# Turning the weights of two key tiles together, in every second slot of the stick-breaking stage

## The chip, the cores and the metric

The kernel runs on one core of a Trainium2 chip. The metric is the device time of one execution in microseconds (us). Five engines work side by side, each through its own list of instructions in order, and they wait for one another with semaphores: TensorE (PE in the profile, its weight loads PEld), VectorE (DVE), ScalarE (ACT), GpSimd (POOL) and SyncE (SP), which here issues the DMA transfers.

## The reference, cut to what matters

One layer of a streaming encoder for 2048 prompt frames and 32 sample frames. The part that the change touches is the stick-breaking attention of the prompt: 8 heads of 64, no softmax.

```python
def stick_breaking(q, k, v, q_pos, k_pos):
    z = jnp.einsum('bqhd,bkhd->bhqk', q, k).astype(jnp.float32) * (HEAD_DIM ** -0.5)
    mask = k_pos[None, :] < q_pos[:, None]
    log_keep = jnp.where(mask, jax.nn.log_sigmoid(-z), 0.0)
    after = lax.cumsum(log_keep, axis=3, reverse=True) - log_keep
    w = jnp.where(mask, jnp.exp(jax.nn.log_sigmoid(z) + after), 0.0)
    return jnp.einsum('bhqk,bkhd->bqhd', w.astype(v.dtype), v)
```

The weight of a key is sigmoid(z) times the product of sigmoid(-z) over all keys after it. Around it stand an input projection, a sliding-window attention, gates, and `x + mixed @ w_out`.

## The kernel before, in words

The program first norms and projects (norm, window and pair stages), then does the sample frames, and from 712 us on runs the stick-breaking stage, which the change edits. It takes the prompt in four blocks of 512 queries. For each block and head it goes back over the key blocks from the diagonal one (`u.diagonal`) to the first (`u.last`). One head with one query block and one key block is a *unit*: 80 in all, of four *tiles* each, so 320 tiles, numbered c. A diagonal unit has narrower tiles.

A tile goes through six steps on four engines:

1. `front` (PE): two products give scores in `c_score`, L1527 and L1528; a diagonal unit adds a mask, L1530.
2. `sigmoids` (ACT): *keep*, L1381, and *take*, L1384.
3. `scan` (DVE): the running product from the last key to the first, L1462.
4. `weigh` (POOL): take times the scanned product, into `c_weight`, L1356.
5. `turn` (PE): transposes of 128x128, L1539. Steps 1 to 4 are by 128 queries, and a turn is by 128 keys, so it reads all four query tiles of its unit. ACT copies the turned tile rounded into `c_w_hi` (`back_hi`, L1392), and DVE puts the rest into `c_w_lo` (`back_lo`, L1470).
6. `mix` (PE): the weights' two parts times the values, summed over a head in `c_o`, L1552 and L1553. At a head's end ACT and DVE take the sum out (`finish`, L1397 and L1475), and the first `mix` of the next head waits for that (`o_ready`).

The order on each engine is written out by hand, by a loop over *slots*. In slot c TensorE does `turn(c)`, `front(c + 8)`, one to five *flow* pieces, and `mix(c - 3)`. The flow is other matrix work woven in: the gates' projection and the output projection (L1572 to L1574, a step of three products with 512 or 272 columns), and transposes of its results (L1587). ACT does in slot c `back_hi(c)` and `sigmoids(c + 8)`, then the flow's copies and, every four to eight slots, the rounding of new flow weights (L1130). DVE does `scan(c + 7)`, `back_lo(c)`, then the flow's sums; POOL does `weigh(c + 5)`, the gating product (L1363) and the rest of the flow weights (L1134).

The turned tiles alternate between two PSUM banks, `turn_ps[c % 2]`, and so do the scores. The waits that matter here:

- `turn(c)` waits for `back_lo(c - 2)` (which frees its bank), and with the first tile of a unit for all four `weigh` of the unit.
- `front(c)` waits for `scan(c - 2)`.
- `back_hi(c)` waits for `turn(c)` and for `mix(c - 4)`.
- The first `weigh` of unit u waits until the last tile of unit u - 2 is turned; take of tile c waits for `weigh(c - 4)`.

Of the kernel before, what the change touches and what calls it, by code (L numbers as in the profile page):

```python
# [254 lines left out]
def after(eng, signal, count):  # L255

    if count > 0:
        eng.wait_ge(signal, count)
# [727 lines left out]
SB_SLOTS = PHASE_START[NSB]  # L986
# [165 lines left out]
def stick_breaking_stage(nc, s, flow):  # L1152
# [13 lines left out]
    with ExitStack() as ctx:  # L1166
# [349 lines left out]
        def _(pe):  # L1516
            def front(c):
                u, j = UNITS[c // QB], c % QB
                after(pe, take_ready, c - 1)
                after(pe, scanned, c - 1)  # L1520
                if j == 0:
                    if u.diagonal:
                        pe.wait_ge(flow.q_in[u.e], 32 * (u.head // 2 + 1))
                    pe.wait_ge(flow.k_in[u.number % 3], 16 * (u.number // 3 + 1))
                n = u.width(j)
                out, keys = score[c % 2][:, 0:n], flow.k[u.number % 3][:, 0:n]
                pe.matmul(out, flow.q[u.e][:, 0, P * j:P * j + P], keys, start=True, stop=False)  # L1527
                last = pe.matmul(out, flow.q[u.e][:, 1, P * j:P * j + P], keys, start=False, stop=not u.diagonal)  # L1528
                if u.diagonal:
                    last = pe.matmul(score[c % 2][:, n - P:n], s.ident_r[:], s.causal_r[:], start=False, stop=True)  # L1530
                last.then_inc(scored, 1)

            def turn(c):
                u, n = UNITS[c // QB], c % QB
                if n == 0:
                    pe.wait_ge(weighted, 4 * u.number + 4)
                after(pe, lo_ready, c - 1)
                for j in range(n if u.diagonal else 0, QB):
                    last = pe.transpose(turn_ps[c % 2][:, j * P:(j + 1) * P],  # L1539
                                        weight[:, u.number % 2, j, n * P:(n + 1) * P], s.ident[:])  # L1540
                last.then_inc(turned, 1)

            def mix(c):
                u, n = UNITS[c // QB], c % QB
                pe.wait_ge(lo_ready, c + 1)
                if n == 0:
                    if u.diagonal:
                        after(pe, o_ready, u.head)
                    pe.wait_ge(flow.v_in[u.number % 3], 16 * (u.number // 3 + 1))
                cols = slice(P * n if u.diagonal else 0, SB)  # L1550
                v = flow.v[u.number % 3][:, n, :]
                pe.matmul(o_ps[:, cols], v, w_hi[n][:, cols], start=(u.diagonal and n == 0), stop=False)  # L1552
                pe.matmul(o_ps[:, cols], v, w_lo[n][:, cols], start=False, stop=(u.last and n == QB - 1)).then_inc(mixed, 1)  # L1553

            def flow_atom(p, nth):

                dt = MIX_ORDER[nth]
                j = p.chunk
                cols = slice(p.first, p.first + p.cols)
                if p.kind == GATE:  # L1560
                    xh, xl = (a[min(p.b, 1)][:, dt, cols] for a in (flow.hi, flow.lo))
                else:
                    xh, xl = (a[mix_home(p.b)][:, dt, cols] for a in (flow.hi, flow.lo))
                if nth == 0:
                    after(pe, flow_free[p.bank], p.turn)
                    pe.wait_ge(flow.w_lo_ready, j + 1)
                    if p.kind == GATE and p.m == 0 and p.b:
                        pe.wait_ge(flow.x_in[p.b], 16 * 2 * DT)
                if p.kind == OUT and p.m == 0:
                    pe.wait_ge(m_lo_ready, DT * p.b + nth + 1)  # L1570
                out = flow_ps[p.bank][:, 0:p.cols]
                pe.matmul(out, flow.w_hi[j % 3][:, dt, :], xh, start=(nth == 0), stop=False)  # L1572
                pe.matmul(out, flow.w_hi[j % 3][:, dt, :], xl, start=False, stop=False)  # L1573
                last = pe.matmul(out, flow.w_lo[j % 3][:, dt, :], xh, start=False, stop=(nth == DT - 1))  # L1574
                if nth == DT - 1:
                    last.then_inc(flow_ready, 1)

            def flow_rows(p):

                after(pe, flow_free[p.bank], p.turn)  # L1580
                sources = [outs[p.b, p.m, f] for f in ((0, 272) if p.b == 0 else (0,))] if p.kind == ROWS else \
                          [outs[p.b, DT - 1, 272]]
                for src in sources:
                    pe.wait_ge(flow_free[src.bank], src.turn + 1)
                for j in range(QB):
                    if p.kind == ROWS:
                        last = pe.transpose(flow_ps[p.bank][:, j * P:(j + 1) * P], part[p.m % 2][:, j * P:(j + 1) * P],  # L1587
                                            s.ident[:])
                    else:
                        last = pe.transpose(flow_ps[p.bank][0:NS, j * P:(j + 1) * P], ys[:, QB * p.m + j, :], s.ident[:])  # L1590
                last.then_inc(flow_ready, 1)

            for c in range(SLOT_0, SLOTS_ALL):
                if 0 <= c < SB_SLOTS:
                    turn(c)
                if c + 8 < SB_SLOTS:
                    front(c + 8)
                for p in pieces:
                    for nth, slot in enumerate(p.slots):
                        if slot == c:  # L1600
                            if p.kind in (GATE, OUT):
                                flow_atom(p, nth)
                            else:
                                flow_rows(p)
                if 0 <= c - 3 < SB_SLOTS:
                    mix(c - 3)
# [347 lines left out]
```

## Time and profile before

| | |
|---|---|
| median of 3 runs | 1534.36 us (1531.79 to 1536.13) |
| profiled execution | 1534.72 us, span in the trace 1532.9 us |
| PE busy over the span | 1392.3 us (91%) |
| DVE, ACT, POOL busy | 1031.1 us (67%), 896.0 us (58%), 580.6 us (38%) |
| granted TensorE clock, mean | 0.96 |

Busy is the time in which an engine has an instruction running. The matmuls of PE overlap, so two that start 0.23 us apart are each shown as 0.39 us long. The times in the rows below are from the start of the span.

### The profile page before, as it was taken

How to read it: one execution, taken by the hardware profiler on the slowest of the kernel's cores; microseconds unless marked ns; L12 is line 12 of the kernel's file. 1: busy time of each engine (PE TensorE's matmuls, PEld its weight loads, DVE VectorE, ACT ScalarE, POOL GpSimd, SP SyncE). 2: the span in 40 equal slices, each digit the busy share in tenths (PEclk: the TensorE clock that was granted, in tenths of full speed). 3: DMA queues.
4: the chain of work that ended last, by engine and by line, in shares of the span. 5: the costliest groups of instructions: out<-in, count | busy, mean ns of one | idle time of the engine just before them, and what ended most of it. 6: DMA issues, size and time to landing. Idle time of an engine off the chain costs nothing.

```text
span 1532.9 us, 23564 instructions
## 1 busy us (share of the span) xinstructions
PE 1392.3 (91%) x7794; PEld 1182.7 (77%) x7794; DVE 1031.1 (67%) x1467; ACT 896.0 (58%) x1927; POOL 580.6 (38%) x481
## 2 busy tenths in 40 slices
PE   3699986998999999868999999899999999999988
PEld 2588875887877887748987899687888777777767
DVE  5467752767567666544777766688887898888931
ACT  7433332555545555325776676577777787777831
POOL 1010111110110101024467645566565666655742
PEclk9699997999999999968999999999999999999999
DMA  5045544554545555364978677655675655445533
GB/s 223 28 180 222 194 139 143 165 155 139 160 131 157 156 150 140 122 171 125 270 239 250 181 217 198 179 175 165 191 213 153 191 173 144 128 124 149 170 119 110
DMA packets 267487, 254.37 MB, mean 166 GB/s; under 512 B 22401, under 2 KB 198137, under 8 KB 266601
## 3 DMA queue, kind: packets, MB, share of 16 engines
q1 hardware_dynamic: 267368, 252.88, 55.5%
q8 instruction: 64, 1.05, 0.3%
q14 instruction: 55, 0.44, 0.1%
HBM read 165.84 MB, written 87.16 MB: 165 GB/s over the span
## 4 chain that ended last, share of the span: by engine, by line
PE 38%; issue 7%; POOL 5%; ACT 2%; DVE 1%; DMA 1%; POOLq 0%; SPq 0%; DVEq 0%; ACTq 0%
PE c_flow L1572 6%; PE c_flow L1574 6%; PE c_flow L1573 6%; PE c_turn L1539 6%; POOL c_weight L1356 3%; PE c_score L1527 3%; PE c_o L1552 3%; PE c_score L1528 3%; PE c_o L1553 3%; POOL f_w_lo L1134 1%; ACT cache_k_rows L1384 1%; PE c_flow L1587 1%; DVE f_kept L1462 1%; POOL c_o_in L1363 1%; ACT f_keep L1381 1%
## 5 line engine op out<-in xcount | busy, mean ns | idle before, releaser
L1356 POOL TENSOR_TENSOR c_weight<-cache_k_rows,f_kept 128x512 f32<-128x512 f32 (+2 forms) x320 | 306.6, 985 | 91.6 <-PE c_turn L1539 82.1
L1462 DVE TENSOR_TENSOR_SCAN f_kept<-f_keep,f_kept,c_score 128x513 f32<-128x513 f32 x192 | 245.1, 1276 | 45.4 <-ACT cache_k_rows L1384 39.0
L1470 DVE TENSOR_TENSOR c_w_lo<-c_turn,c_w_hi 128x512 fp32r<-128x512 f32 (+1 forms) x320 | 191.8, 599 | 80.6 <-ACT c_w_hi L1392 77.8
L1392 ACT ACTIVATE c_w_hi<-c_turn 128x512 fp32r<-128x512 f32 (+1 forms) x320 | 171.4, 536 | 127.3 <-PE c_turn L1539 123.9
L1134 POOL TENSOR_TENSOR f_w_lo<-f_w_raw,f_w_hi 128x1024 fp32r<-128x1024 f32 x64 | 153.5, 2400 | 211.2 <-ACT f_w_hi L1130 211.2
L248 POOL TENSOR_TENSOR w_w_lo<-w_w_raw,w_w_hi 128x1024 fp32r<-128x1024 f32 x18 | 44.0, 2444 | 392.5 <-ACT w_w_hi L243 392.3
L1384 ACT ACTIVATE cache_k_rows<-c_score 128x512 f32<-128x512 f32 (+2 forms) x320 | 173.1, 541 | 33.2 <-POOL c_weight L1356 33.0
L276 PE MATMUL b_ps<-XH,w_w_hi 128*128 128x512 f32 (+1 forms) x480 | 178.3, 371 | 11.4 <-PEq L290 11.4
L1539 PE MATMUL c_turn<-ident,c_weight 128*128 128x128 f32 x1088 | 173.5, 275 | 5.9 <-POOL c_weight L1356 3.0
L1381 ACT ACTIVATE f_keep<-c_score 128x512 f32<-128x512 f32 (+2 forms) x320 | 171.0, 534 | 10.5 <-PE c_score L1530 5.2
L278 PE MATMUL b_ps<-XH,w_w_lo 128*128 128x512 f32 (+1 forms) x480 | 170.3, 355 | 0.0
L277 PE MATMUL b_ps<-XL,w_w_hi 128*128 128x512 f32 (+1 forms) x480 | 170.1, 354 | 0.0
L1539 PEld LDWEIGHTS c_turn<-ident,c_weight 128*128 128x128 f32 x1088 | 134.6, 141 | 38.4 <-POOL c_weight L1356 6.4
L1527 PE MATMUL c_score<-f_k,f_q 128*128 128x512 f32 (+2 forms) x320 | 142.9, 447 | 13.8 <-DVE f_kept L1462 8.2
L1552 PE MATMUL c_o<-c_w_hi,f_v 128*128 128x512 f32 (+1 forms) x320 | 118.5, 370 | 16.0 <-issue 15.5
L1572 PE MATMUL c_flow<-XH,f_w_hi 128*128 128x272 f32 (+1 forms) x384 | 130.1, 339 | 0.0
L1462 DVE TENSOR_TENSOR_SCAN f_kept<-f_keep,c_score 128x128 f32<-128x128 f32 (+3 forms) x128 | 104.4, 816 | 36.9 <-ACT cache_k_rows L1384 32.1
L1574 PE MATMUL c_flow<-XH,f_w_lo 128*128 128x272 f32 (+1 forms) x384 | 125.3, 326 | 0.0
L1573 PE MATMUL c_flow<-XL,f_w_hi 128*128 128x272 f32 (+1 forms) x384 | 125.1, 326 | 0.0
L1528 PE MATMUL c_score<-f_k,f_q 128*128 128x512 f32 (+2 forms) x320 | 117.9, 368 | 0.0
L1553 PE MATMUL c_o<-c_w_lo,f_v 128*128 128x512 f32 (+1 forms) x320 | 117.6, 367 | 0.0
L1572 PE MATMUL c_flow<-f_hi,f_w_hi 128*128 128x512 f32 x256 | 104.9, 410 | 7.8 <-DVE f_lo L1496 6.3
(227 smaller groups left out, 3152.0 us busy)
## 6 DMA issues: line engine op xcount, KB each, us to landing
f_k<-k_parts SPq DMA_DIRECT2D x80, 256.0 KB, 4.1
f_v<-v_parts SPq DMA_DIRECT2D x80, 256.0 KB, 2.7
f_q<-q_parts SPq DMA_DIRECT2D x64, 256.0 KB, 5.3
f_w_raw<-in_w_in SPq DMA_DIRECT2D x32, 512.0 KB, 4.2
f_w_raw<-in_w_out SPq DMA_DIRECT2D x32, 512.0 KB, 4.1
w_w_raw<-in_w_in SPq DMA_DIRECT2D x18, 512.0 KB, 4.7
x_rows<-in_x_prompt SPq DMA_DIRECT2D x4, 2048.0 KB, 10.1
k_parts<-b_part SPq DMA_DIRECT2D x16, 512.0 KB, 2.8
```

Source lines behind the costliest of these rows:

```text
L276: pe.matmul(out, w.hi[n][:, dt, :], xh, start=(dt == 0), stop=False)
L1356: pool.tensor_tensor(weight[:, u.number % 2, j, 0:n], take[:, j, 0:n], kept[:, j, 1:n + 1], ALU.mult).then_inc(weighted, 1)
L1381: act.activation(keep[:, c % 2, 0:n], score[c % 2][:, 0:n], ACT.Sigmoid, scale=-SCALE)\
L1384: act.activation(take[:, j, 0:n], score[c % 2][:, 0:n], ACT.Sigmoid, scale=SCALE)\
L1392: act.activation(w_hi[n][:, cols], turn_ps[c % 2][:, cols], ACT.Copy).then_inc(hi_ready, 1)
L1462: dve.tensor_tensor_scan(kept[:, j, down], keep[:, c % 2, down], score[c % 2][:, 0:1].to_broadcast([P, n]), above, ALU.mult, ALU.bypass).t ...
L1470: dve.tensor_tensor(w_lo[n][:, cols], turn_ps[c % 2][:, cols], f32(w_hi[n][:, cols]), ALU.subtract).then_inc(lo_ready, 1)
L1527: pe.matmul(out, flow.q[u.e][:, 0, P * j:P * j + P], keys, start=True, stop=False)
L1539: last = pe.transpose(turn_ps[c % 2][:, j * P:(j + 1) * P], weight[:, u.number % 2, j, n * P:(n + 1) * P], s.ident[:])
L1572: pe.matmul(out, flow.w_hi[j % 3][:, dt, :], xh, start=(nth == 0), stop=False)
L1573: pe.matmul(out, flow.w_hi[j % 3][:, dt, :], xl, start=False, stop=False)
L1574: last = pe.matmul(out, flow.w_lo[j % 3][:, dt, :], xh, start=False, stop=(nth == DT - 1))
```

## The change

In even slots TensorE turns tile c and then tile c + 1; in odd slots it turns none. Everything else in TensorE's list, and all of the other engines' lists, stays as it is, and no wait is added to or taken from an instruction. `turn(c + 1)` is the same list of transposes with the same waits, but it stands ahead of `front(c + 8)`, of the flow work of slot c, of `mix(c - 3)` and of whatever slot c has else, all of which stood ahead of it before.

```diff
@@ -1591,8 +1591,9 @@
             for c in range(SLOT_0, SLOTS_ALL):
-                if 0 <= c < SB_SLOTS:
+                if 0 <= c < SB_SLOTS and c % 2 == 0:
                     turn(c)
+                    turn(c + 1)
                 if c + 8 < SB_SLOTS:
                     front(c + 8)
                 for p in pieces:
```

The first place is slots 236 and 237 on TensorE, full-width tiles of the last query block, before the change. `c_turn0` and `c_turn1` are the two banks of turned tiles, `c_score0` and `c_score1` those of the scores, and the semaphore `c_lo_ready` counts `back_lo`, `c_scanned` counts `scan`.

```order
5920 L1539 MATMUL c_turn0<-ident,c_weight 128x128 [waits c_lo_ready,c_weighted]
5921 L1539 MATMUL c_turn0<-ident,c_weight 128x128 x3
5922 L1527 MATMUL c_score0<-f_k1,f_q1 128x512 [waits f_k_in1,c_scanned,c_take_ready]
5923 L1528 MATMUL c_score0<-f_k1,f_q1 128x512
5924 L1572 MATMUL c_flow1<-f_hi,f_w_hi0 128x512
5925 L1573 MATMUL c_flow1<-f_lo,f_w_hi0 128x512
5926 L1574 MATMUL c_flow1<-f_hi,f_w_lo0 128x512
5927 L1552 MATMUL c_o<-c_w_hi1,f_v1 128x512 [waits c_lo_ready]
5928 L1553 MATMUL c_o<-c_w_lo1,f_v1 128x512
5929 L1539 MATMUL c_turn1<-ident,c_weight 128x128 [waits c_lo_ready]
5930 L1539 MATMUL c_turn1<-ident,c_weight 128x128 x3
5931 L1527 MATMUL c_score1<-f_k1,f_q1 128x512 [waits c_scanned,c_take_ready]
```

The same place on TensorE in the changed kernel:

```order
5920 L1539 MATMUL c_turn0<-ident,c_weight 128x128 [waits c_lo_ready,c_weighted]
5921 L1539 MATMUL c_turn0<-ident,c_weight 128x128 x3
5922 L1539 MATMUL c_turn1<-ident,c_weight 128x128 [waits c_lo_ready]
5923 L1539 MATMUL c_turn1<-ident,c_weight 128x128 x3
5924 L1527 MATMUL c_score0<-f_k1,f_q1 128x512 [waits f_k_in1,c_scanned,c_take_ready]
5925 L1528 MATMUL c_score0<-f_k1,f_q1 128x512
5926 L1572 MATMUL c_flow1<-f_hi,f_w_hi0 128x512
5927 L1573 MATMUL c_flow1<-f_lo,f_w_hi0 128x512
5928 L1574 MATMUL c_flow1<-f_hi,f_w_lo0 128x512
5929 L1552 MATMUL c_o<-c_w_hi1,f_v1 128x512 [waits c_lo_ready]
5930 L1553 MATMUL c_o<-c_w_lo1,f_v1 128x512
5931 L1527 MATMUL c_score1<-f_k1,f_q1 128x512 [waits c_scanned,c_take_ready]
```

The four transposes of `turn(237)`, with their wait for `back_lo(235)`, have moved from behind `mix(233)` to ahead of `front(244)`; the score products, the flow step and the mix of slot 236 now come after it, and slot 237 begins with its score products.

The second place is the end of a head on TensorE, slots 110 and 111 before the change: 4660 and 4661 are the last mix of a head, 4671 the first of the next, which waits for `c_o_ready`.

```order
4660 L1552 MATMUL c_o<-c_w_hi3,f_v2 128x512 [waits c_lo_ready]
4661 L1553 MATMUL c_o<-c_w_lo3,f_v2 128x512
4662 L1539 MATMUL c_turn1<-ident,c_weight 128x128 [waits c_lo_ready]
4663 L1527 MATMUL c_score1<-f_k2,f_q1 128x512 [waits c_scanned,c_take_ready]
4664 L1528 MATMUL c_score1<-f_k2,f_q1 128x512
4665 L1572 MATMUL c_flow1<-f_hi,f_w_hi2 128x512
4666 L1573 MATMUL c_flow1<-f_lo,f_w_hi2 128x512
4667 L1574 MATMUL c_flow1<-f_hi,f_w_lo2 128x512
4668 L1572 MATMUL c_flow1<-f_hi,f_w_hi2 128x512
4669 L1573 MATMUL c_flow1<-f_lo,f_w_hi2 128x512
4670 L1574 MATMUL c_flow1<-f_hi,f_w_lo2 128x512
4671 L1552 MATMUL c_o<-c_w_hi0,f_v0 128x512 [waits f_v_in0,c_o_ready,c_lo_ready]
```

In the changed kernel TensorE's list from `turn(110)` on reads:

```order
4653 L1539 MATMUL c_turn0<-ident,c_weight 128x128 [waits c_lo_ready]
4654 L1539 MATMUL c_turn0<-ident,c_weight 128x128
4655 L1539 MATMUL c_turn1<-ident,c_weight 128x128 [waits c_lo_ready]
4656 L1527 MATMUL c_score0<-f_k2,f_q1 128x512 [waits c_scanned,c_take_ready]
4657 L1528 MATMUL c_score0<-f_k2,f_q1 128x512
4658 L1572 MATMUL c_flow1<-f_hi,f_w_hi2 128x512
4659 L1573 MATMUL c_flow1<-f_lo,f_w_hi2 128x512
4660 L1574 MATMUL c_flow1<-f_hi,f_w_lo2 128x512
4661 L1552 MATMUL c_o<-c_w_hi3,f_v2 128x512 [waits c_lo_ready]
4662 L1553 MATMUL c_o<-c_w_lo3,f_v2 128x512
4663 L1527 MATMUL c_score1<-f_k2,f_q1 128x512 [waits c_scanned,c_take_ready]
4664 L1528 MATMUL c_score1<-f_k2,f_q1 128x512
```

The single transpose that stood between the last mix of the old head and the first of the new one now stands ahead of both.

## Rows read from the trace of the kernel before

**Rows 1.** Windows: length; busy of PE, PEld, DVE, ACT, POOL; clock; DMA

```profile
963.00:1194.00 231.00, 218.64 (x1167) 180.20 (x1165) 180.87 (x225) 169.88 (x336) 140.02 (x120) 0.98 0.61 179
1194.00:1472.00 278.00, 260.75 (x1408) 212.12 (x1407) 240.98 (x290) 215.22 (x424) 181.95 (x154) 1.00 0.52 152
...
990.00:995.00 5.00, 2.42 (x7) 1.80 (x8) 3.66 (x4) 2.70 (x6) 3.60 (x5) 0.50 0.65 210
```

**Rows 2.** Waits, 712 to 1533 us: who for whom, us in total, times, longest

```profile
ACT c_w_hi L1392 <- PE c_turn L1539: 123.9, 175, 2.9
POOL c_weight L1356 <- PE c_turn L1539: 82.1, 35, 6.2
DVE c_w_lo L1470 <- ACT c_w_hi L1392: 77.8, 113, 5.0
...
ACT cache_k_rows L1384 <- POOL c_weight L1356: 33.0, 38, 2.0
...
PE c_o L1552 <- issue: 15.5, 17, 2.0
...
PE c_score L1527 <- DVE f_kept L1462: 8.2, 11, 2.6
...
PE c_turn L1539 <- POOL c_weight L1356: 3.0, 6, 0.9
```

**Rows 3.** Timeline of PE around `turn(111)`, a single transpose

```profile
1007.36 0.27 PE L1539 MATMUL c_turn<-ident,c_weight 128*128 128x128 f32 x1
...
1007.38 0.48 PE L1527 MATMUL c_score<-f_k,f_q 128*128 128x512 f32 x1
...
1007.70 0.40 PE L1528 MATMUL c_score<-f_k,f_q 128*128 128x512 f32 x1
```

**Rows 4.** Timeline, slots 236 to 238: PE, ACT and DVE

```profile
1293.48 0.60 PE L1539 MATMUL c_turn<-ident,c_weight 128*128 128x128 f32 x4
...
1294.15 0.39 PE L1528 MATMUL c_score<-f_k,f_q 128*128 128x512 f32 x1
...
1297.61 0.60 PE L1539 MATMUL c_turn<-ident,c_weight 128*128 128x128 f32 x4
...
1294.60 0.59 ACT L1381 ACTIVATE f_keep<-c_score 128x512 f32<-128x512 f32 x1
1295.08 0.61 ACT L1384 ACTIVATE cache_k_rows<-c_score 128x512 f32<-128x512 f32 x1
...
1295.78 1.28 DVE L1462 TENSOR_TENSOR_SCAN f_kept<-f_keep,f_kept,c_score 128x513 f32<-128x513 f32 x1 [0.34 <-ACT cache_k_rows L1384]
1296.98 0.66 DVE L1470 TENSOR_TENSOR c_w_lo<-c_turn,c_w_hi 128x512 fp32r<-128x512 f32 x1
```

**Rows 5.** Timeline, slots 46 and 318: PE, and the back_lo needed

```profile
822.80 0.60 PE L1539 MATMUL c_turn<-ident,c_weight 128*128 128x128 f32 x4
...
827.81 0.47 PE L1527 MATMUL c_score<-f_k,f_q 128*128 128x512 f32 x1 [1.92 <-DVE f_kept L1462]
...
823.93 0.69 DVE L1470 TENSOR_TENSOR c_w_lo<-c_turn,c_w_hi 128x512 fp32r<-128x512 f32 x1 [3.19 <-ACT c_w_hi L1392]
...
1469.39 0.66 PE L1539 MATMUL c_turn<-ident,c_weight 128*128 128x128 f32 x4
...
1469.85 0.68 DVE L1470 TENSOR_TENSOR c_w_lo<-c_turn,c_w_hi 128x512 fp32r<-128x512 f32 x1
```

**Rows 6.** Timeline at the head's end in slot 111: DVE, then PE

```profile
1009.53 0.68 DVE L1475 TENSOR_TENSOR c_o_sum<-c_o,c_o_sum 64x512 f32<-64x512 f32 x1
...
1010.32 0.47 PE L1552 MATMUL c_o<-c_w_hi,f_v 128*128 128x512 f32 x1 [0.84 <-issue]
```

**Rows 7.** Timeline of POOL, one unit and a half of the last block

```profile
1350.28 2.41 POOL L1134 TENSOR_TENSOR f_w_lo<-f_w_raw,f_w_hi 128x1024 fp32r<-128x1024 f32 x1 [4.39 <-ACT f_w_hi L1130]
1352.64 5.30 POOL L1356 TENSOR_TENSOR c_weight<-cache_k_rows,f_kept 128x512 f32<-128x512 f32 x5
1360.56 1.85 POOL L1356 TENSOR_TENSOR c_weight<-cache_k_rows,f_kept 128x128 f32<-128x128 f32 x3 [2.61 <-PE c_turn L1539]
```

## The prediction

> **What bounds the kernel now.** I read the windows first. In the last query block of the stick-breaking stage (1194 to 1472 us, 128 slots) PE is busy 260.75 of 278 us, DVE 240.98 and ACT 215.22; in the block before it the shares are 95%, 78% and 74% [rows 1]. So TensorE sets the pace, and in the last block DVE is close behind: there is little room for PE and DVE to get out of step. Then the waits. PE waits little in the stage: 15.5 us at the ends of heads (shown as "issue"; the wait is for the head's sum, below), 8.2 us for a scan, 3.0 us for POOL before a turn. The large waits are on engines that are ahead: POOL for a turn 82.1 us, ACT for a turn 123.9 us of the same kind (of which nothing here depends), DVE for ACT's rounded half 77.8 us [rows 2]. Last I read the timeline slot by slot, for what a turned tile waits for and how long before the turn that was ready.
>
> **The transposes themselves: nothing.** Grouping could pay if each switch between transposes and products cost something. At turn(111), one transpose, the second score product starts 0.34 us after it; at turn(236), four transposes, 0.67 us after the first [rows 3, 4]. Three more transposes cost 0.33 us, 0.11 each, and 0.34 - 0.11 = 0.23 is what one 512-column product takes to the start of the next. The line goes through zero: no fixed cost per group, so 160 fewer groups save 0. A turn of four is 0.45 us, and it is done once, before and after.
>
> **The wait that moves.** turn(c + 1) needs back_lo(c - 1). That used to be asked at the start of slot c + 1, a slot of some 2.1 us later; now it is asked right behind turn(c). On DVE back_lo(c - 1) comes directly after scan(c + 6), so TensorE must now wait in slot c until DVE has done that scan and one subtraction more, where before only front(c + 8) asked for the scan alone. Queued behind the wait are front(c + 8), the flow step and mix(c - 3), and for the scores ACT, DVE and POOL wait in turn.
>
> I went through all 159 even slots from c = 2 and compared the end of back_lo(c - 1) with the end of turn(c) (start plus 0.11 per transpose). It is late in 25: 1 in the second query block, 4 in the third, 20 in the last, 1.38 + 5.37 + 8.86 = 15.6 us in all. The first is slot 46: turn at 822.80, ended 823.24, subtraction ended 824.62, 1.38 late. The last is slot 318: 1469.39 + 0.44 against 1470.53, 0.70 late [rows 5]. In 31 more it is ready by less than 0.45 us.
>
> Term 1, the 25 late places. They don't all cost. In six of them front(c + 8) already waits in the same slot for the scan just ahead of that subtraction, 4.65 us, and at slots 46 (1.38) and 232 (0.45) a longer wait follows in the next slot and shrinks by as much: 1.92 us at 827.81 [rows 5]. That leaves 15.6 - 4.65 - 1.83 = 9.1. Where several follow within a few slots it is one lag of DVE seen again, and TensorE pays for its largest once: 2.5 less. **+6.6 us**; bounds 0 (all trades against later waits) and 15.6.
>
> Term 2, the shift. In even slots front(c + 8) now starts 0.45 us later, behind the second turn, and the subtraction that the next pair needs hangs on it. Slots 236 to 238 show the loop: scores end 1294.15 + 0.39 = 1294.54, take ends 1295.69, the scan starts 1295.78, the subtraction ends 1297.64, 3.10 us after the scores; turn(238) starts 1297.61 [rows 4]. With the scores 0.45 us later the subtraction ends 1298.09, and turn(239) could go at 1297.61 + 0.45 = 1298.06. With 0.06 us for the semaphore (as from the scores' end to ACT at 1294.60) TensorE stalls 0.1 us, in the plainest pair of full slots (4.13 us a pair), and more wherever DVE has an extra sum or a take is late. For the 31 places with little room, 0.51 less the room of each sums to 7.6 us, and where ACT or DVE was behind anyway the later scores are hidden: I take half, 3.8. The late places get the shift too, at most 25 x 0.5 = 12.7; most of them are late because DVE or ACT is behind, so I take 1.7. **+5.5 us**; bounds 0 and 20.3. In odd slots front moves not at all: what its slot loses at the head the slot before gained.
>
> Term 3, the ends of heads. The last mix of a head is in an even slot and the first of the next in the odd one behind it. ACT copies, DVE adds until 1010.21, PE starts at 1010.32 after 0.84 idle [rows 6]. The one transpose between the two mixes now stands ahead of both, so it no longer covers 0.11 us of this. 17 such waits [rows 2]: **+1.9 us**; bounds 0 and 2.
>
> Term 4, what comes back. ACT may round an odd tile at once when its slot begins, some 0.45 us earlier than now, so DVE gets odd tiles earlier where it waits for ACT: a part of the 77.8 us [rows 2]. POOL's first weigh of a unit is released a slot earlier. Little of this reaches PE, since take and scan of odd tiles hang on scores that don't move. **-3 us**, an estimate; bounds 0 and -12 (the faster rival).
>
> The DMAs, ACT's, DVE's and POOL's lists are untouched. Sum: 6.6 + 5.5 + 1.9 - 3 = +11 us, on the profiled execution 1534.72 + 11 = 1545.7. That execution is 0.36 us above the median, so **1545.4 us** against 1534.36.
>
> **Rivals.** *The waits only trade* (0.23). DVE's list is the same and PE waited for its scans anyway; a stall lets DVE, ACT and POOL catch up, and the next stall shrinks. For it: slot 46, and the other seven places above. Against it: PE waits only 8.2 us for scans in all [rows 2], less than the 15.6 us that comes, so at least the rest is new. Terms 1 and 2 at a quarter, 3.0, plus 1.9, less the 3: about +2, 1536 us.
>
> *Faster: POOL released early* (0.10). The 82.1 us in which POOL waits for the last turn of a unit [rows 2] end a slot sooner. If that made weights and so takes earlier, it would eat ACT's 33.0 us of waits for POOL, then PE's 3.0 for POOL and 8.2 for scans [rows 2], together 11.2; less term 3, and with terms 1 and 2 traded away, -9: 1525 us. Against it: in the last block POOL is late just after it took the flow weights at 1350.28, held 4.39 us by ACT and not by a turn, then runs five weighs on end; where it waits for a turn, 2.61 us before 1360.56, it is ahead [rows 7]. It decides if more than about a third of ACT's 38 waits come from POOL runs that a turn released; I found none in the last block.
>
> *Slower by the clock* (0.04). The granted clock is 1.00 over the whole last block, with a turn's 0.45 us in each slot; it was seen at 0.50 (1.2 GHz) around 990 to 995 us, where PE was busy 2.42 of 5 us [rows 1]. If pairs of turns with a stall behind turn(c) let it fall once more for two stretches of ten microseconds, that is 10 us on top: 1556 us. The Trainium skill, "TensorE: Matmul & The Clock Gate", in its part on PE-mode transpose, says that transposes don't count as busy as matmuls do, which would speak against eight in a row. The window of the last block, a fifth of it transposes at full clock, doesn't bear that out, and the share stays the same.
>
> My forecast, a new wait of TensorE for DVE, has the rest, 0.63.
>
> **How the numbers follow.** Within 0.3% of the old median (4.6 us, about what a measurement tells from no change) is 1529.8 to 1539.0. The forecast's own range is 1537 (term 2 nearly nothing) to 1557 (term 1 at 9, term 2 at twice, nothing back); a tenth of it falls under 1539. Slower: 0.57 + 0.04 and 0.05 of the trading rival, 0.66. Same: 0.06 + 0.16 + 0.02 of the faster rival, 0.24. Faster: 0.08 + 0.02 of trading, 0.10. The range takes in the trading rival and stops short of the faster one: 1532 to 1557.
>
> **What the changed profile would show.** Right: in PE's waits a large group c_turn <- DVE c_w_lo, 10 us or more, nearly all after 963 us and in even slots, while c_score <- DVE shrinks to a few us; the wait "issue" before c_o 1 to 2 us larger; POOL's wait for a turn well under 82 us with no gain on PE; the last block some 8 us longer than now, the first two no longer. The transposes still 0.11 us apart. Wrong: c_turn <- DVE stays under 5 us, or it comes and as much goes elsewhere; or the waits of POOL and ACT fall and PE's with them; or the clock falls in the last block.

## The result

The changed kernel takes **1545.31 us** (median of 4 runs, 1544.43 to 1547.6) against 1533.97 us before (4 runs on the same chip, 1531.79 to 1536.13): ratio 1.0076, 95% interval 1.0058 to 1.0094. It is slower by some 11 us; the forecast was 1545.4. The profiled execution took 1545.52 us, with a span of 1543.7 us.

Busy time over the span, from the page of the changed kernel, hardly moved against the table of before. TensorE does the same work over a longer time:

```profile
PE 1395.5 (90%) x7794; PEld 1187.0 (77%) x7794; DVE 1030.5 (67%) x1467; ACT 902.6 (58%) x1927; POOL 581.3 (38%) x481
```

The waits of the changed kernel, 712 to 1545 us (who for whom, us in total, times, longest), which answer to [rows 2]:

```profile
ACT c_w_hi L1392 <- PE c_turn L1539: 55.2, 88, 2.0
POOL c_weight L1356 <- PE c_turn L1539: 31.0, 18, 3.9
DVE c_w_lo L1470 <- ACT c_w_hi L1392: 67.3, 96, 3.9
...
ACT cache_k_rows L1384 <- POOL c_weight L1356: 30.2, 37, 2.1
ACT f_keep L1381 <- PE c_score L1528: 28.3, 72, 2.4
...
PE c_o L1552 <- issue: 17.9, 19, 2.3
...
PE c_turn L1539 <- DVE c_w_lo L1470: 15.9, 20, 3.5
...
PE c_turn L1539 <- POOL c_weight L1356: 2.3, 5, 0.8
...
PE c_score L1527 <- DVE f_kept L1462: 1.3, 4, 0.4
```

In the trace of before, the same wait of TensorE for DVE's subtraction was:

```profile
PE c_turn L1539 <- DVE c_w_lo L1470: 2.7, 2, 2.6
```

Three things are to be seen. TensorE has a new wait, a turn that waits for DVE's subtraction: 15.9 us in 20 places, against 2.7 us in 2. Its wait for a scan fell from 8.2 to 1.3 us, so about 6.9 us of the new wait were there already under another name. And POOL's wait for a turn fell from 82.1 to 31.0 us, ACT's for a turn from 123.9 to 55.2, while ACT's wait for POOL only went from 33.0 to 30.2: those engines get turned tiles earlier and it brings TensorE nothing.

Where the time went is told by marks, each the start of an instruction: the first scores of the stage (at 696.2 us in the trace of before, so the stage starts somewhat earlier than the 712 us given at its description), `turn(192)`, which opens the last query block, and the last `mix`. "Last block" is from `turn(192)` to the last `mix`. "To the end" runs on to the end of the span, some 60 us later.

| us | first scores to turn(192) | last block | first scores to the end |
|---|---|---|---|
| before | 498.0 | 278.8 | 836.7 |
| changed | 497.9 | 288.3 | 846.6 |

The two rows that bound the last block, in the trace of before and in that of the changed kernel:

```profile
1194.18 0.60 PE L1539 MATMUL c_turn<-ident,c_weight 128*128 128x128 f32 x4
...
1472.97 0.50 PE L1552 MATMUL c_o<-c_w_hi,f_v 128*128 128x512 f32 x1 [0.36 <-DVE c_w_lo L1470]
```

```profile
1195.01 0.93 PE L1539 MATMUL c_turn<-ident,c_weight 128*128 128x128 f32 x7
...
1483.32 0.50 PE L1552 MATMUL c_o<-c_w_hi,f_v 128*128 128x512 f32 x1
```

The last block is 9.5 us longer. The stretch before it is as long as it was, but that hides a loss of about 2 us, as the traces taken again will show. Tile by tile, the mix of a tile comes 0.3 us earlier than before at tile 96, then 0.9 us later at tile 192, 4.9 at 224, 7.7 at 256, 8.6 at 288 and 10.4 at 319: a loss spread over the whole block. The granted clock has a small part in it. The windows that answer to [rows 1] show 0.99 in both blocks, where before had 0.98 and 1.00:

```profile
963.00:1194.00 231.00, 217.29 (x1161) 180.21 (x1159) 179.59 (x224) 170.06 (x334) 139.58 (x119) 0.99 0.60 178
1195.00:1483.00 288.00, 266.30 (x1409) 215.40 (x1407) 242.24 (x291) 218.36 (x424) 181.79 (x153) 0.99 0.49 148
```

One place shows the mechanism at its plainest. The timeline of the changed kernel from slot 260 on, where turns 260 and 261 stand together:

```profile
1352.79 1.03 PE L1539 MATMUL c_turn<-ident,c_weight 128*128 128x128 f32 x8
...
1353.58 0.48 PE L1527 MATMUL c_score<-f_k,f_q 128*128 128x512 f32 x1
...
1353.90 0.40 PE L1528 MATMUL c_score<-f_k,f_q 128*128 128x512 f32 x1
...
1354.34 0.60 ACT L1381 ACTIVATE f_keep<-c_score 128x512 f32<-128x512 f32 x1 [0.31 <-PE c_score L1528]
1354.83 0.59 ACT L1384 ACTIVATE cache_k_rows<-c_score 128x512 f32<-128x512 f32 x1
1355.51 1.28 DVE L1462 TENSOR_TENSOR_SCAN f_kept<-f_keep,f_kept,c_score 128x513 f32<-128x513 f32 x1 [0.77 <-ACT cache_k_rows L1384]
1356.71 0.67 DVE L1470 TENSOR_TENSOR c_w_lo<-c_turn,c_w_hi 128x512 fp32r<-128x512 f32 x1
...
1356.58 0.60 PE L1539 MATMUL c_turn<-ident,c_weight 128*128 128x128 f32 x4
...
1357.43 0.66 PE L1539 MATMUL c_turn<-ident,c_weight 128*128 128x128 f32 x4 [0.25 <-DVE c_w_lo L1470]
```

Eight transposes, then the scores; ACT waits 0.31 us for them and DVE 0.77 us for ACT; the subtraction behind that scan ends at 1357.38, and the second turn of the next pair starts at 1357.43, 0.85 us after the first, where four transposes take 0.44. Before the change that subtraction had ended 0.07 us before the first turn did. Measured like this, from start to start and less 0.109 us per transpose, TensorE loses 20.7 us between the two turns of a pair in the whole stage, in 49 places: 2.1 in the second query block, 5.2 in the third and 13.5 in the last. That is more than the wait rows show, since the modelled ends of matmuls hide the start of each gap.

### The profile page after: what moved, and what is told of

Same layout as the page of the kernel before. It is cut to its first block, busy times and chain, and to the rows that moved or that the text cites. A ratio compares the mean times of both kernels' runs of the same rounds, so it can differ in the third digit from the quotient of the medians.

```text
span 1543.7 us, 23564 instructions
## 1 busy us (share of the span) xinstructions
PE 1395.5 (90%) x7794; PEld 1187.0 (77%) x7794; DVE 1030.5 (67%) x1467; ACT 902.6 (58%) x1927; POOL 581.3 (38%) x481
## 4 chain that ended last, share of the span: by engine, by line
PE 38%; issue 6%; POOL 4%; ACT 4%; DVE 2%; DMA 1%; SPq 0%; DVEq 0%; ACTq 0%; POOLq 0%
PE c_flow L1572 6%; PE c_turn L1539 6%; PE c_flow L1573 6%; PE c_flow L1574 6%; PE c_score L1527 3%; PE c_score L1528 3%; PE c_o L1552 3%; PE c_o L1553 3%; POOL c_weight L1356 2%; ACT cache_k_rows L1384 1%; ACT f_keep L1381 1%; POOL c_o_in L1363 1%; PE c_flow L1587 1%; ACT c_w_hi L1392 1%; POOL f_w_lo L1134 1%
## 5 line engine op out<-in xcount | busy, mean ns | idle before, releaser
L1392 ACT ACTIVATE c_w_hi<-c_turn 128x512 fp32r<-128x512 f32 (+1 forms) x320 | 171.5, 536 | 101.6 <-PE c_turn L1539 55.2
L1384 ACT ACTIVATE cache_k_rows<-c_score 128x512 f32<-128x512 f32 (+2 forms) x320 | 172.1, 538 | 30.4 <-POOL c_weight L1356 30.2
L1539 PE MATMUL c_turn<-ident,c_weight 128*128 128x128 f32 x1088 | 153.9, 276 | 18.6 <-DVE c_w_lo L1470 15.9
L1539 PEld LDWEIGHTS c_turn<-ident,c_weight 128*128 128x128 f32 x1088 | 126.7, 141 | 46.6 <-DVE c_w_lo L1470 24.2
L1527 PE MATMUL c_score<-f_k,f_q 128*128 128x512 f32 (+2 forms) x320 | 131.7, 412 | 6.1 <-PEq L1616 3.9
L1552 PE MATMUL c_o<-c_w_hi,f_v 128*128 128x512 f32 (+1 forms) x320 | 118.3, 370 | 18.1 <-issue 17.9
L1528 PE MATMUL c_score<-f_k,f_q 128*128 128x512 f32 (+2 forms) x320 | 117.9, 369 | 0.0
## 6 DMA issues: line engine op xcount, KB each, us to landing
x_rows<-in_x_prompt SPq DMA_DIRECT2D x4, 2048.0 KB, 10.3
```

Of the source, the lines that this page charges most:

```text
L1384: act.activation(take[:, j, 0:n], score[c % 2][:, 0:n], ACT.Sigmoid, scale=SCALE)\
L1392: act.activation(w_hi[n][:, cols], turn_ps[c % 2][:, cols], ACT.Copy).then_inc(hi_ready, 1)
L1539: last = pe.transpose(turn_ps[c % 2][:, j * P:(j + 1) * P], weight[:, u.number % 2, j, n * P:(n + 1) * P], s.ident[:])
```

## The experiments

The expectations name three theories. W: the time goes where TensorE waits for DVE's subtraction behind an early turn, and late scores feed back into that wait. S: the late scores alone starve ACT and DVE. T: transposes in a group, or the clock, cost TensorE itself. In the tables "last block" and "to the end" are the two stretches above. Since one trace each is compared, I first give what two runs of the same kernel differ by.

**Both kernels again.** No edit.

> The kernel before once more with a profile, to see how far two traces of one kernel differ: first score to the end of the span 836.7 us in the first, last query block 278.8. I expect within 1.5 and 0.7 us of these.

> The changed kernel once more with a profile, for the same reason: 846.6 us and 288.3 us in the first, within 1.5 and 0.7 us of these.

| | first to turn(192) | last block | to the end | lost in the last block |
|---|---|---|---|---|
| before, again | 495.7 | 280.2 | 836.1 | 29.2 |
| changed, again | 497.5 | 289.0 | 846.4 | 38.1 |

"Lost" is the last block less what its matmuls take at their plain spacing from start to start, about 251 us in every kernel; the first traces gave 27.7 and 37.5. The stretch to the end repeats within 0.6 us, the last block within 1.4 (more than I had expected), and the first three blocks only within 2.3. The single times, 1532.85 and 1540.46 us, differ from the medians by more: the first scores start anywhere from 689 to 701 us, behind stages that no edit touches. Means of the two are used for "to the end" below: 836.4 and 846.5.

Much of this scatter goes with the granted clock. In the last block, the second trace of before has a stretch of 3.4 us at a granted 0.50 (1.2 of 2.4 GHz), which the first lacks. Its row, in the order of [rows 1]:

```profile
1237.00:1240.00 3.00, 3.00 (x11) 2.51 (x11) 3.00 (x4) 1.48 (x3) 2.28 (x2) 0.50 0.70 197
```

It comes just after TensorE stood idle for 2.02 us at a head's end. The first trace of before has the same wait, 2.04 us at the same place, and its clock stays at 1.00. So such a stretch comes and goes between runs of one kernel, and a trace is best compared with one that spent as long at 0.50 in the same blocks:

| order of turns | first to turn(192), us of it at 0.50 | last block, us of it at 0.50 |
|---|---|---|
| old: before | 498.0, 20.0 | 278.8, 0 |
| old: before, again | 495.7, 12.9 | 280.2, 3.4 |
| old in the first three blocks, pairs in the last (below) | 495.2, 10.1 | 289.4, 3.4 |
| pairs in the first three blocks, old in the last (below) | 498.0, 10.1 | 278.2, 0 |
| pairs: changed | 497.9, 10.1 | 288.3, 3.4 |
| pairs: changed, again | 497.5, 10.1 | 289.0, 3.4 |

Like with like, the pairs cost 8.1 to 8.8 us in the last block (against 280.2) and some 2 us in the first three (497.5 to 498.0 against 495.2, and 496.4 in the kernel with the third bank and the old order, which also has 10.1 us). Traces with the same order and the same time at 0.50 differ by 1.2 us or less. The differences of the last block in brackets below are against the trace of before with the same time at 0.50 there.

The timed runs show it too. Of 34 timed runs of the kernel before on one chip, the 15 with a mean clock up to 0.960 took 1537.9 us on average and the 12 with 0.965 or more 1529.6. A straight line through time and mean clock, the same for an edited kernel and for before, gives each edit's difference "at equal clock". It is an estimate from the timed runs of both kernels, uncertain by about 1.3 us to either side for kernels with 10 runs or more and by up to 2 for those with six.

**The second turn behind the scores.** Turns stay paired in even slots, but `front(c + 8)` stands between them. The edit is shown against the kernel before.

```diff
-                if 0 <= c < SB_SLOTS:
+                if 0 <= c < SB_SLOTS and c % 2 == 0:
                     turn(c)
                 if c + 8 < SB_SLOTS:
                     front(c + 8)
+                if 0 <= c < SB_SLOTS and c % 2 == 0:
+                    turn(c + 1)
```

> In even slots TensorE turns tile c, then does the scores of tile c + 8, then turns tile c + 1; the rest is as in the change. The scores of even slots are no longer late, and the early turn asks for its subtraction 0.46 us later than in the change. Theory W (the time goes where TensorE, behind the early turn, waits for DVE's subtraction of tile c - 1, with the late scores feeding back into that wait): most of it comes back, a few places over half a us late stay, 1535 to 1539 us. Theory S (the late scores of even slots alone starve ACT and DVE, the subtraction wait only shows it): all comes back, 1533 to 1535. Theory T (transposes grouped two and two, or the clock, cost TensorE itself): 1534. If the time stays at 1543 or more, what counts is only that the odd turn stands in the even slot, and W's feedback is wrong.

Ratio 1.0005 (0.9982 to 1.0027), at equal clock -0.5 us; last block 278.5 (-0.3), to the end 835.4. Its waits on TensorE:

```profile
PE c_score L1527 <- DVE f_kept L1462: 7.8, 10, 3.0
...
PE c_turn L1539 <- DVE c_w_lo L1470: 4.3, 5, 2.6
```

The early second turn costs nothing once the scores go ahead of it. POOL's wait for a turn is 30.8 us here too, and no gain is to be seen from that relief either. This removes two causes: the second turn's place a slot earlier, and the flow and mix that now stand behind it. What costs is its place ahead of the scores. Eight transposes in a row are not tested here, since the scores part them; their spacing and the kernel with wait and late scores, below, speak to that.

**The wait alone.** The old order; in even slots TensorE asks behind `turn(c)` for what `turn(c + 1)` would ask.

```diff
                     turn(c)
+                    if c % 2 == 0 and c:
+                        pe.wait_ge(lo_ready, c)
```

> The order of before, with one more wait: in even slots the scores of tile c + 8 also wait until DVE has done the subtraction of tile c - 1. Nothing is moved, so the scores are late only where they wait. Theory W: the late places cost without the feedback of 0.45 us, 4 to 7 us, 1538 to 1541. Theory S: nothing or up to 2 us, 1534 to 1536. Theory T: nothing, 1534.

Ratio 1.0046 (1.0026 to 1.0067), at equal clock +5.8 us, in theory W's range; last block 282.9 (+2.7), to the end 842.1 (+5.7). The scores now wait for the subtraction:

```profile
PE c_score L1527 <- DVE c_w_lo L1470: 8.7, 9, 3.5
...
PE c_score L1527 <- DVE f_kept L1462: 1.9, 5, 0.6
```

The wait costs without any transpose moved, and takes over most of the 8.2 us for scans.

**The scores late alone.** The old order of turns; in even slots, except at the ends of heads, `mix(c - 3)` (0.46 us) goes ahead of `front(c + 8)`. This shifts the scores by what the second turn does, and adds no wait.

```diff
+            def early(c):
+                return c % 2 == 0 and not ((c - 3) % QB == QB - 1 and UNITS[(c - 3) // QB].last)
 ...
+                if 0 <= c - 3 < SB_SLOTS and early(c):
+                    mix(c - 3)
                 if c + 8 < SB_SLOTS:
                     front(c + 8)
 ...
-                if 0 <= c - 3 < SB_SLOTS:
+                if 0 <= c - 3 < SB_SLOTS and not early(c):
                     mix(c - 3)
```

> The order of before, turns where they stood, but in even slots (those at a head's end left out) mix(c - 3) is done before the scores of tile c + 8 instead of at the slot's end, so that these scores start 0.46 us late, as in the change, with no early turn and no new wait. In the trace the last query block (mix of tile 191 to mix of tile 319) took 272.7 us before and 281.9 with the change. Theory W (the late scores cost only because the early turn's subtraction hangs on them): 272 to 275 us there, the whole 1533 to 1537 us. Theory S (the late scores alone starve ACT and DVE): 277 to 282 us there, the whole 1540 us or more.

Ratio 1.005 (1.0026 to 1.0073), at equal clock +3.9 us; last block 281.3 (+1.1), to the end 842.5 (+6.1). By the expectation's own mark, from the mix of tile 191 to that of tile 319, the last block takes 275.2 us, at the edge of what theory W said; the whole time is what theory S said, so neither held. Late scores cost something by themselves, and more of it in the first three blocks (500.3 us, with 20.1 at 0.50, against 498.0 with 20.0), which I can't lay on one wait. The mix itself moved too, so this isn't a pure shift of the scores.

**Wait and late scores together**, the two edits above in one kernel, turns unmoved.

> No turn is moved. In even slots (at the ends of heads without the second part) the wait of e4_wait_only for the subtraction of tile c - 1 is put in, and mix(c - 3) stands between it and the scores of tile c + 8, as in e10_scores_late. Alone, the wait cost 4.1 us in the last query block and the late scores 2.5; the change cost 9.5. Theory W (the two feed each other: the subtraction hangs on scores that are late by its own wait): 8 to 11 us there, as in the change, though all transposes stand where they stood. If the two merely add: 6 to 7. If 5 or less, something else of the pair (the transposes themselves) makes up the difference.

Ratio 1.008 (1.0055 to 1.0105), at equal clock +10.8 us; last block 286.6 (+7.8), to the end 846.8 (+10.4). The loss of the changed kernel is there, within the noise, without a single transpose moved. The wait now shows at the mix, which is first behind it:

```profile
PE c_o L1552 <- issue: 17.1, 17, 2.5
PE c_o L1552 <- DVE c_w_lo L1470: 12.1, 15, 3.5
```

By the expectation's numbers, 7.8 us lies between adding (6 to 7) and feeding each other (8 to 11). Like with like it speaks for feeding: this trace has nothing at 0.50 in the last block and the other two have 3.4 us, and 2.7 + 1.1 = 3.8 us apart stand against 7.8 together, where equal traces differed by at most 1.2. Over the whole nothing of the kind is to be seen: 5.8 + 3.9 = 9.7 us apart against 10.8, at equal clock. That each feeds the other is likely for the last block, then, but it rests on one trace of each kernel.

**By blocks.** The pairs only in the last query block (`c >= PHASE_START[3]`), and only before it.

```diff
+                if 0 <= c < SB_SLOTS and (c < PHASE_START[3] or c % 2 == 0):
                     turn(c)
+                    if c >= PHASE_START[3]:
+                        turn(c + 1)
```

> Turns in pairs only from slot 192 on, the last query block. Theory W: nearly the whole loss is here, where DVE has little room (20 of the 25 late places): the last block takes 280 to 283 us, the whole is 8 to 10 us over the kernel before. A theory in which each pair costs the same wherever it stands (T, or a cost of the switch of banks) gives 64 of 160 pairs, 4 to 5 us.

> Turns in pairs only before slot 192, the first three query blocks, 96 of 160 pairs. Theory W: 0 to 2 us over the kernel before, and the last block 272 to 274 us. A theory in which each pair costs the same gives 6 to 7 us.

| | ratio | at equal clock | last block | to the end | `c_turn` for `back_lo` |
|---|---|---|---|---|---|
| last block only | 1.0065 (1.0033 to 1.0097) | +9.0 us | 289.4 (+9.2) | 843.8 | 10.3 us |
| first three only | 1.0033 (1.0009 to 1.0058) | +2.8 us | 278.2 (-0.6) | 836.4 | 7.1 us |

The expectations count the last block from mix to mix, as above (272.7 us before, 281.9 changed); so counted it takes 283.2 and 272.1 us here, as theory W said to within 0.2. Most of the loss is in the last block, and pairs don't cost the same wherever they stand. The first three blocks cost little, though they have 7.1 us of the new wait: the wait for a scan fell from 8.2 to 3.5 us there. That the stretch to the end is no longer than before, 836.4 us, goes with the clock: at equal time at 0.50 these blocks take some 2 us more (the table above), and the timed runs at equal clock say 2.8. The ratio's 0.3% is less firm than it looks, since the medians are 1534.89 and 1534.29.

**A third bank for turned tiles.** With three banks `turn(c + 1)` asks for `back_lo(c - 2)`, a slot less late. The third is taken from the flow in the last block alone; a control has the same banks and the old order. Two lines of the edit:

```diff
+        turn_bank = lambda c: turn_ps[c % 2] if c < LAST else (turn_ps + [flow_ps[2]])[c % 3]
 ...
-                after(pe, lo_ready, c - 1)
+                after(pe, lo_ready, c - 2 if c >= LAST + 3 else c - 1)
```

> The change, and in the last query block (slots 192 to 319) the turned tiles rotate through three PSUM banks, the third taken from the flow, which there has two instead of three. So in that block turn(c + 1) asks for the subtraction of tile c - 2, not c - 1; the scores of even slots stay 0.45 us late. To be read against e6_banks_plain. Theory W: the difference to e6 is 1 to 4 us (the loss of the first blocks, 1 to 2, and the heads' ends, 1). Theory S and theory T: it stays about 11 us.

> The order of before with the same three banks for turned tiles and two for the flow in the last block: the control of e5. The flow may wait for ACT's copies where its bank comes back sooner, the turns wait less: 1533 to 1542 us. All theories say the same of it; what counts is e5 less this.

| | time, us (before 1536.32) | last block | lost there |
|---|---|---|---|
| pairs, third bank | 1543.46, 1.0059 (1.0037 to 1.0082) | 284.6 | 33.8 |
| old order, third bank | 1539.62, 1.0035 (1.0014 to 1.0056) | 280.8 | 30.0 |

```profile
PE c_turn L1549 <- DVE c_w_lo L1478: 6.8, 4, 3.6
...
PE c_score L1535 <- DVE f_kept L1470: 5.1, 12, 0.7
```

Neither trace has time at 0.50 in the last block. Pairing costs that block 3.8 us over its control instead of 8.1 to 8.8, and all of the 6.8 us of the wait for the subtraction lie before it: in the last block, where the changed kernel has 8.1 us of that wait, there is none. Taking the early wait away takes more than half of the loss there away. What is left, 3.8, is more than late scores alone cost there (+1.1); I have no trace that tells the rest. Over the whole the difference is less clear: 3.8 us by the medians, as theory W said, but 5.9 at equal clock and 8.3 to the end in the two traces (845.1 and 836.8), since the first three blocks are paired in one and not in the other.

**The ends of heads.** In the slot of a head's last mix, that mix goes ahead of `front`: `early(c)` is now true at the ends of heads and nowhere else.

```diff
+            def early(c):
+                return (c - 3) % QB == QB - 1 and UNITS[(c - 3) // QB].last
```

> The order of before, but the last mix of each head stands ahead of the scores of its slot instead of at the slot's end, so that the head's sum is out before the next head's first mix asks for it. By term 3 read the other way (what stands between the last mix and the next head's first covers the wait), the 15.5 us of waits before c_o should fall to under 3, and 5 to 14 us come off: 1520 to 1529 us, unless waits for scans take their place (the scores of these slots start 0.2 to 0.4 us late), in which case 1532 to 1536.

Ratio 1.003 (1.0008 to 1.0053), at equal clock +3.9 us; last block 282.2 (+2.0). The expectation missed: the wait did not go, and it is longer than the 15.5 us of before:

```profile
PE c_o L1552 <- issue: 19.4, 19, 2.0
```

The timeline of before at such a place shows why:

```profile
1342.44 0.59 ACT L1397 ACTIVATE c_o_sum<-c_o 64x512 f32<-64x512 f32 x1
1342.46 1.28 DVE L1462 TENSOR_TENSOR_SCAN f_kept<-f_keep,f_kept,c_score 128x513 f32<-128x513 f32 x1 [0.27 <-issue]
...
1343.77 0.68 DVE L1475 TENSOR_TENSOR c_o_sum<-c_o,c_o_sum 64x512 f32<-64x512 f32 x1
...
1344.56 0.47 PE L1552 MATMUL c_o<-c_w_hi,f_v 128*128 128x512 f32 x1 [0.87 <-issue]
```

ACT's copy is done at 1343.03, but DVE's addition stands behind a scan that runs until 1343.74. So some 0.7 of the 0.87 us for which TensorE waits go to that scan, by an estimate from these rows, and its own last mix is not what holds it. The scan is that of the tile whose scores come in the slot of the last mix; here they come behind that mix, later than before, and the wait grew by 3.9 us.

**The head's sum out early.** The same, and DVE's `finish` ahead of that scan, ACT's one slot earlier, behind `back_hi`.

```diff
@@ ACT @@
-                if n == 3 and 1 <= number <= len(UNITS) and UNITS[number - 1].last:
-                    finish(UNITS[number - 1])
                 if 0 <= c < SB_SLOTS:
                     back_hi(c)
+                if n == 2 and 1 <= number <= len(UNITS) and UNITS[number - 1].last:
+                    finish(UNITS[number - 1])
@@ DVE @@
-                if 0 <= c + 7 < SB_SLOTS:
-                    scan(c + 7)
                 if n == 3 and 1 <= number <= len(UNITS) and UNITS[number - 1].last:
                     finish(UNITS[number - 1])
+                if 0 <= c + 7 < SB_SLOTS:
+                    scan(c + 7)
```

> The order of before, with the head's sum taken out earlier: the last mix of a head as in e9_head_mix_early, ACT's copy of the sum ahead of the sigmoids of its slot, and DVE's addition ahead of the scan of the next slot. In e9 the wait before c_o did not fall (19.4 us), since DVE's addition stands behind a scan that waits for the new scores. If that is what holds it: c_o <- issue under 4 us, 5 to 12 us faster than before, 1523 to 1530. If the takes and scans that come 0.6 us later at each head take it back: 1532 to 1537.

Ratio **0.9926** (0.9898 to 0.9954), 1519.56 us (6 runs, 1514.47 to 1525.74) against 1530.46: faster than both kernels, by 10.9 us, within the 5 to 12 expected. At equal clock it is 13.8 us. From the first scores to the end it takes 822.6 us, also 13.8 less, of it 6.1 in the last block (272.7 against 278.8). The wait at the head's end is gone. Three instructions moved here (the mix, ACT's copy and DVE's addition), and no run moves the last two one by one. In the timeline of before the copy is done 0.7 us before the scan is, which points at the addition. The timeline at the same head shows it ahead of the scan, and the next mix with no wait:

```profile
PE c_o L1552 <- issue: 0.5, 1, 0.5
```

```profile
1334.19 0.40 PE L1553 MATMUL c_o<-c_w_lo,f_v 128*128 128x512 f32 x1
...
1334.62 0.59 ACT L1397 ACTIVATE c_o_sum<-c_o 64x512 f32<-64x512 f32 x1
...
1335.57 0.68 DVE L1475 TENSOR_TENSOR c_o_sum<-c_o,c_o_sum 64x512 f32<-64x512 f32 x1
1336.42 1.28 DVE L1462 TENSOR_TENSOR_SCAN f_kept<-f_keep,f_kept,c_score 128x513 f32<-128x513 f32 x1 [0.17 <-issue]
...
1336.86 0.39 PE L1552 MATMUL c_o<-c_w_hi,f_v 128*128 128x512 f32 x1
```

## Why the prediction was right

The forecast and its mechanism held: a new wait of TensorE for DVE, mostly in the last block, +11 us where +11.3 was measured. The terms were less exact than the sum, and that they add up to within 0.1 us of the measured time is luck.

- **The transposes cost nothing.** Right. The second score product starts 0.34, 0.67 and 1.11 us after the first of one, four and eight transposes (1007.70, 1294.15 and 1353.90 us in the rows), 0.11 us for each. And wait plus late scores make the loss with none moved.
- **Term 1, the early wait (+6.6).** The mechanism is shown by the wait alone, the third bank and the scores between. Its size alone is +5.8 us at equal clock, +2.7 of it in the last block. The places were right too: 17.0 of the 20.7 us lost between the turns of a pair lie in the 25 named. That part of it would trade against the wait for scans was right as well: 6.9 us where 4.65 was taken, 5.5 in the traces taken again.
- **Term 2, the shift (+5.5).** Late scores on top of the wait cost 10.8 - 5.8 = 5.0 us at equal clock, and 7.8 - 2.7 = 5.1 in the last block, where the loop that this term describes was to work. So its size held. But scores that are late with no such wait cost too, 3.9 us at equal clock and only 1.1 of them in the last block. So there is a second route, which the prediction left out and which my traces don't name.
- **Term 3, the ends of heads (+1.9).** The size is about right (15.5 to 17.9 us, and 15.5 to 18.1 in the traces taken again, a little over its bound of 2), the reason wrong. The prediction had the transpose between the two mixes cover a part of the wait. The wait hangs on DVE's addition, which stands behind a scan: with the last mix moved early and no transpose moved it grew to 19.4 us, and with copy and addition moved early it went. The scan is later when the scores of its slot are, which the kernel with the last mix early did without a turn; that it is the same link in the changed kernel was argued, not tried.
- **Term 4, what comes back (-3).** Not found. The second turn behind the scores has these reliefs and lies at -0.5 us at equal clock, 1.3 to either side. It has 1.6 us more of the wait for the subtraction than before, though, so a small gain may be hidden.
- **The range.** Its lower end was said to be the sum with term 2 nearly nothing. That gives 6.6 + 0 + 1.9 - 3 = 5.5 us, 1540, not 1537. The interval of the measured time lies above both.
- **The faster rival** fell: the 51 us that POOL no longer waits left ACT's wait for POOL at 30.2 us, and the kernel with that relief and no cost gains nothing that can be told from zero. **The trading rival** was right for some 6 us, and near to right for the first three blocks, which cost some 2 us for 7.1 us of new wait; it was wrong for the last block. **The clock** rival fell: in the last block 3.4 us at 0.50 cost at most half of that, 1.7 us, of TensorE's time, and one of the two traces of before has the same. The Trainium skill ("TensorE: Matmul & The Clock Gate", PE-mode transpose) has it that transposes don't count as busy. Here TensorE did eight in a row in every pair of full slots and its granted clock over the last block was 0.99, as in one trace of before, so this made no difference.
- **The signs.** `c_turn` for `c_w_lo` 15.9 us (10 or more foretold), `c_score` for a scan 1.3 (a few), the wait at heads +2.4 (1 to 2), the last block +8.1 to +8.8 (some 8), no gain on TensorE from POOL.

## What to carry to other kernels

On an engine that runs in order, moving an instruction up also moves its wait up, in front of all that it passes. List for each such place when the awaited work ends and when the wait would now be asked; where the room is under the new stall, ask what the instructions behind it feed. Here the scores feed ACT, DVE and POOL, and keeping them ahead of the early wait made the same early turns free. A wait that one engine has at the end of a group of work can hang on an unrelated instruction that stands ahead of the awaited one in another engine's list: look there before moving anything on the waiting engine. And before laying a difference of 1 or 2 us between two traces on an edit, see how long each spent at the lower clock.

## What the runs showed that was not expected

- Grouping or splitting transposes and products on TensorE shows neither cost nor gain at this size: 0.109 us from start to start for 128x128 in fours and in eights.
- Removing 15.0 us of waits at the ends of heads (15.5 to 0.5) brought 13.8 us from the first scores on and 10.9 by the medians of the timed runs, nearly one for one. The waits of a new kind that the changed kernel brought did so less neatly: some 6 of its 15.9 us were traded for waits that it had.
- Moving one mix of 0.46 us ahead of the scores, with no wait added, cost 0.5% (3.9 us at equal clock), though TensorE's own wait rows look nearly as before (17.4 us at heads, 8.0 for scans). Where that time sits no view here tells.
- Whether TensorE falls to 0.50 after a wait at a head's end changes from run to run of one kernel. With mean clocks from 0.957 to 0.969, times of the kernel before on one chip spread from 1525 to 1541 us.
